# Attention scores with the low key products in two row halves, and the compressed values and the overlap table as one operand

## What is computed

```python
p_c = jax.nn.softmax(jnp.where(mask_c, s_c, NEG_INF), axis=-1) * mask_c
o_cmp = jnp.einsum('bgrqj,bjgd->bqgrd', p_c, vcmp)
...
imp = jnp.einsum('bgrqj,jk->bgqk', p_c, jnp.asarray(overlap.astype(np.float32)))
...
_, sel_idx = lax.top_k(imp, n_pick)
...
s = (jnp.einsum('bqgrd,bgqkd->bgrqk', qb, kg)
     - slopes[None, :, :, None, None] * dist.astype(f32))
p = jax.nn.softmax(jnp.where(dist >= 0, s, NEG_INF), axis=-1)
o_sel = jnp.einsum('bgrqk,bgqkd->bqgrd', p, vg)
...
sw = jnp.einsum('bqgrd,bkgd->bgrqk', qb, kwb) - slopes[..., None, None] * dw.astype(f32)
```

## Time and profile before

| | |
|---|---|
| Time, three runs | 4975.93, 4977.47, 4987.32 us; median 4977.47 |
| Profiled execution | 4984.44 us, of it 4982.9 us from the first to the last instruction |
| TensorE matmul busy | 87% of the span |
| VectorE, ScalarE, GpSimd busy | 55%, 41%, 15% |
| Attention proper | from 2024 to 3077 us of the span |
| TensorE's mean granted clock | 0.922 of full speed |

### The profile page before, as it was taken

One profiled execution on the slowest core, in us unless ns is written; L12 is line 12 of the kernel. 1 busy time (PEld: TensorE's weight loads), 2 busy tenths in 40 slices (PEclk: granted clock), 3 DMA queues, 4 the chain that ended last, 5 costly groups with the idle time before them and its releaser, 6 DMA issues. The chain is left out here.

```text
span 4982.9 us, 66879 instructions
## 1 busy us (share of the span) xinstructions
PE 4327.2 (87%) x24608; PEld 3592.7 (72%) x24609; DVE 2748.0 (55%) x4353; ACT 2039.0 (41%) x3193; POOL 729.3 (15%) x599
## 2 busy tenths in 40 slices
PE   6999999999999995788888876799635999999699
PEld 5887887888788773566666764688534888888577
DVE  2655655556567562576666654443225654557465
ACT  2433332233223221455555553101225655557465
POOL 0111111111122130211111110000012100001110
PEclk9999999999999997899999986899657999999899
DMA  4332322233222214000000001423217865669742
GB/s 138 108 87 74 107 81 62 86 109 87 65 74 61 67 43 104 25 11 14 17 15 17 14 22 55 140 94 115 92 59 293 314 249 214 245 256 344 286 145 98
DMA packets 440438, 558.72 MB, mean 112 GB/s; under 512 B 38908, under 2 KB 299004, under 8 KB 439148
## 3 DMA queue, kind: packets, MB, share of 16 engines
q1 hardware_dynamic: 387892, 451.51, 27.6%
q0 software_dynamic: 19072, 59.86, 3.2%
q10 hardware_dynamic: 33232, 44.10, 2.7%
HBM read 445.05 MB, written 110.35 MB: 111 GB/s over the span
## 5 line engine op out<-in xcount | busy, mean ns | idle before, releaser
L434 POOL TENSOR_TENSOR fr_Lm<-fr_M,fr_join 128x512 f32<-128x512 f32 x224 | 370.9, 1673 | 1493.2 <-DVE fr_M L1043 963.4
L462 PE MATMUL fr_fb<-fr_hT_h,fr_w_h 128*128 128x512 f32 (+1 forms) x1312 | 528.3, 403 | 16.6 <-DVEq L1004 10.8
L462 PE MATMUL fr_fb<-fr_hT_r,fr_w_h 128*128 128x512 f32 (+1 forms) x1312 | 527.4, 402 | 0.0
L462 PE MATMUL fr_fb<-fr_hT_h,fr_w_r 128*128 128x512 f32 (+1 forms) x1312 | 526.3, 401 | 0.0
L855 DVE TENSOR_TENSOR fr_w_r<-fr_w_raw,fr_w_h 128x1024 fp32r<-128x1024 f32 (+1 forms) x164 | 209.6, 1278 | 409.7 <-ACT fr_w_h L683 409.4
L1781 DVE TENSOR_TENSOR aq_p_lo<-aq_t_bank,aq_p_hi 128x512 fp32r<-128x512 f32 x412 | 281.4, 690 | 271.5 <-ACT aq_p_hi L1671 270.1
L1671 ACT CAST aq_p_hi<-aq_t_bank 128x512 fp32r<-128x512 f32 x412 | 238.9, 585 | 377.5 <-PE aq_t_bank L1585 375.4
L707 ACT COPY fr_zs<-fr_fb 128x512 f32<-128x512 f32 (+1 forms) x148 | 87.0, 588 | 585.0 <-PE fr_fb L462 584.6
L462 PEld LDWEIGHTS fr_fb<-fr_hT_h,fr_w_h 128*128 128x128 f32 (+1 forms) x1312 | 246.9, 188 | 74.7 <-DVEq L1004 11.3
L134 PE MATMUL ex_gu<-ex_gate_w,ex_xT 128*128 128x512 f32 x1176 | 288.3, 401 | 11.5 <-DVE ex_xT L2407 11.4
L134 PE MATMUL ex_yps<-ex_down_w,ex_hidT 128*128 128x512 f32 x1176 | 287.6, 400 | 2.6 <-DVE ex_hidT L2423 2.6
(11 more groups left out here) (438 smaller groups left out, 9957.8 us busy)
## 6 DMA issues: line engine op xcount, KB each, us to landing
ex_raw<-in_w_exp_gate_up SPq DMA_DIRECT2D x64, 2048.0 KB, 10.9
fr_w_raw<-in_w_in SPq DMA_DIRECT2D x160, 512.0 KB, 3.8
ex_raw<-in_w_exp_down SPq DMA_DIRECT2D x32, 2048.0 KB, 11.1
s_z<-fr_zs SPq DMA_DIRECT2D x160, 256.0 KB
s_rows<-ex_y ACTq DMA_DIRECT2D x50, 512.0 KB, 4.3
mx_mg<-s_z SPq DMA_DIRECT2D x16, 1024.0 KB, 7.8
fr_zc<-s_z SPq DMA_DIRECT2D x15, 903.0 KB, 6.8
fr_x_t<-in_x SPq DMA_DIRECT2D x16, 512.0 KB, 4.8
```

The costliest lines, as they stand in the source:

```text
L434: pool.tensor_tensor(Lm[:, g, :, :], M[:, 4 * g:4 * g + 4, 0, :], join[:, lev:lev + 1, :].to_broadcast([P, HG, CH]), ALU.mult).then_inc(l_ ...
L462: ins = pe.matmul(bank[0:cols_, :], (w_h, w_h, w_r)[p][:, k, c, 0:cols_].bitcast(F32R), (hT_h, hT_r, hT_h)[p][:, c, :].bitcast(F32R), star ...
```

## The change

**Scores.** A run is always split into two halves by columns, each half in a bank of its own. Both halves are multiplied with `k_hi` as before, with all 128 rows. The products with `k_lo` now use the rounded query alone: half 0 of the columns with rows 0 to 63 of the array, half 1 with rows 64 to 127. A new tile `q_hh` holds the rounded query in all rows for this. `take_q` has one more copy. `mask` reads and writes the two halves with one instruction.

**Fronts.** `overlap` is now part of `vcmp` (two copies, one for each group), so `out` has one product of 96 columns for each head. The sum over heads is made by a `tensor_reduce` in `select`.

**The SEL mask.** `t_sel` is gone. `bias` first adds `sel` to a ramp of one element for each block, then this to the distances within a block (`near`), and masks the last 128 columns with `affine_select`.

```diff
+        CMP_OUT = N_SEL + HD
+        vcmp = kp.sb("vcmp", [P, G, CMP_OUT])
...
+            q_hh = st.sb("q_hh", [P, 2, G, R, P])
...
-                    pool.tensor_copy(whole(q_s, every).bitcast(F32R), raw(every)).then_inc(q_high, 1)
-                    pool.wait_ge(q_high, o + 1)
-                    pool.tensor_tensor(whole(q_s, rest).bitcast(F32R), raw(rest), whole(q_s, rest), ALU.subtract).then_inc(q_ok, 1)
+                    pool.tensor_copy(whole(q_hh, every).bitcast(F32R), raw(every)).then_inc(q_high, 1)
+                    pool.tensor_copy(whole(q_s, top_).bitcast(F32R), raw(top_)).then_inc(q_high, 1)
+                    pool.wait_ge(q_high, 2 * o + 2)
+                    pool.tensor_tensor(whole(q_s, rest).bitcast(F32R), raw(rest), whole(q_hh, rest), ALU.subtract).then_inc(q_ok, 1)
...
+                    pool.tensor_tensor(base[:, 0:blocks], ramp[:, N_SEL - blocks:N_SEL], sel[:, f % SELS, 0:blocks], ALU.add).then_inc(base_ok, 1)
+                    pool.wait_ge(base_ok, 2 * f + 1)
                     pool.tensor_tensor(tg[:, 0:keys].rearrange("p (n b) -> p n b", n=blocks),
-                                       t_sel[:, S - t * P:S - t * P + keys].rearrange("p (n b) -> p n b", n=blocks),
-                                       sel[:, f % SELS, 0:blocks].rearrange("p (n o) -> p n o", o=1).to_broadcast([P, blocks, SEL_BLOCK]),
-                                       ALU.add).then_inc(tg_ok, 1)
+                                       near[:, :].rearrange("p (o b) -> p o b", o=1).to_broadcast([P, blocks, SEL_BLOCK]),
+                                       base[:, 0:blocks].rearrange("p (n o) -> p n o", o=1).to_broadcast([P, blocks, SEL_BLOCK]),
+                                       ALU.add).then_inc(base_ok, 1)
+                    pool.wait_ge(base_ok, 2 * f + 2)
+                    pool.affine_select(out=tg[:, t * P:keys], in_=tg[:, t * P:keys], compare_op=ALU.is_ge, fill=NEG, base=0,
+                                       pattern=[[-1, P]], channel_multiplier=1).then_inc(tg_ok, 1)
...
-                step(pool.memset(overlap[:, :], 1.0))
-                masked(overlap[:, :], [[-4, N_SEL]], 0, 1, 0.5)
...
+                for g in range(G):
+                    overlap = vcmp[:, g, 0:N_SEL]
+                    step(pool.memset(overlap, 1.0))
+                    masked(overlap, [[-4, N_SEL]], 0, 1, 0.5)
...
-                step(pool.iota(t_sel[:, :], [[1, w]], base=-S, channel_multiplier=-1, allow_small_or_imprecise_dtypes=True))
-                masked(t_sel[:, :], [[-1, w]], S, 1, NEG)
+                step(pool.iota(near[:, :], [[1, SEL_BLOCK]], base=0, channel_multiplier=-1, allow_small_or_imprecise_dtypes=True))
+                step(pool.iota(ramp[:, :], [[SEL_BLOCK, N_SEL]], base=P - S, channel_multiplier=0, allow_small_or_imprecise_dtypes=True))
...
                         for h in range(R):
-                            pe.matmul(misc[:, R * HD:R * HD + N_SEL], pct[0:N_CMP, h, :], overlap[0:N_CMP, :],
-                                      start=h == 0, stop=h == R - 1)
-                        for h in range(R):
-                            ins = pe.matmul(misc[:, h * HD:(h + 1) * HD], pct[0:N_CMP, h, :], vcmp[0:N_CMP, k, :], start=True, stop=True)
+                            ins = pe.matmul(misc[:, h * CMP_OUT:(h + 1) * CMP_OUT], pct[0:N_CMP, h, :], vcmp[0:N_CMP, k, :], start=True, stop=True)
...
-                    key = F.low(u) * P + at
-                    for c in range(0, wide, 512):
-                        size = min(512, wide - c)
-                        dst = s_bank[:, i % 2, c:c + size]
-                        for n, k in enumerate((k_hi, k_lo)):
-                            ins = pe.matmul(dst, q_s[:, t % 2, g, h, :].bitcast(F32R),
-                                            k[:, b, g, key + c:key + c + size].bitcast(F32R), start=n == 0, stop=n == 1)
+                    key, half = F.low(u) * P + at, wide // 2
+                    for c in range(2):
+                        pe.matmul(s_bank[:, i % 2, 512 * c:512 * c + half], q_s[:, t % 2, g, h, :].bitcast(F32R),
+                                  k_hi[:, b, g, key + c * half:key + (c + 1) * half].bitcast(F32R), start=True, stop=False)
+                    for c in range(2):
+                        own = slice(c * HD, (c + 1) * HD)
+                        ins = pe.matmul(s_bank[:, i % 2, 512 * c:512 * c + half], q_hh[own, t % 2, g, h, :].bitcast(F32R),
+                                        k_lo[own, b, g, key + c * half:key + (c + 1) * half].bitcast(F32R), start=False, stop=True)
...
-                    dve.tensor_tensor(imp[:, :], misc[:, R * HD:R * HD + N_SEL], keep_t[:, at], ALU.mult).then_inc(imp_ok, 1)
+                    dve.tensor_reduce(imp[:, :], misc[:, 0:R * CMP_OUT].rearrange("p (h n) -> p n h", h=R)[:, 0:N_SEL, :],
+                                      AX.X, ALU.add).then_inc(imp_ok, 1)
                     dve.wait_ge(imp_ok, f + 1)
+                    v.link(dve.tensor_tensor(imp[:, :], imp[:, :], keep_t[:, at], ALU.mult))
...
-                    dve.tensor_tensor_reduce(out=sc_of(u)[:, h, at:at + wide], in0=s_bank[:, i % 2, 0:wide], in1=table,
+                    dve.tensor_tensor_reduce(out=halves(sc_of(u)[:, h, at:at + wide]),
+                                             in0=s_bank[:, i % 2, :].rearrange("p (b n) -> p b n", b=2)[:, :, 0:wide // 2], in1=halves(table),
                                              scale=-SLOPES[g * R + h], scalar=least[:, u % 4, 0, h:h + 1] if at else HIGHEST,
                                              op0=ALU.add, op1=ALU.min, accum_out=slot).then_inc(s_read, 1)
```

More of the change, by code:

```diff
@@ L1380, in _ @@
                 for g in range(G):
-                    dve.tensor_copy(vcmp[0:N_CMP, g, :], out[0:N_CMP, (2 + g) * P:(2 + g) * P + HD]).then_inc(out_ok, 1)
+                    dve.tensor_copy(vcmp[0:N_CMP, g, N_SEL:CMP_OUT], out[0:N_CMP, (2 + g) * P:(2 + g) * P + HD]).then_inc(out_ok, 1)
                 dve.wait_ge(out_ok, 3)
@@ L1388, in stage_nsa @@
             QF, Y = 3, F.Y_RING
-            t_sel, t_win, t_cmp = st.sb("t_sel", [P, S + P]), st.sb("t_win", [P, WK]), st.sb("t_cmp", [P, 256])
+            t_win, t_cmp = st.sb("t_win", [P, WK]), st.sb("t_cmp", [P, 256])
+            near, ramp, base = st.sb("near", [P, SEL_BLOCK]), st.sb("ramp", [P, N_SEL]), st.sb("base", [P, N_SEL])
             rows_ok = st.sb("rows_ok", [P, 1])
             keep_t, force_t = st.sb("keep_t", [P, 64]), st.sb("force_t", [P, 64])
-            overlap, pair = st.sb("overlap", [P, N_SEL]), st.sb("pair", [P, HD])
+            pair = st.sb("pair", [P, HD])
             q_raw = st.sb("q_raw", [P, G, R, P])
             qf, q_s = st.sb("qf", [P, QF, R, P]), st.sb("q_s", [P, 2, G, R, P])
+            q_hh = st.sb("q_hh", [P, 2, G, R, P])
             pc, pct = st.sb("pc", [P, R, P]), st.sb("pct", [P, R, P])
@@ L1414, in stage_nsa @@
                 st.sem(n) for n in ("s_made", "s_read", "exp_ok", "turned", "hi_ok", "lo_ok", "pv_made", "ot_ok"))
-            misc_made, misc_read, cexp_ok, inv_ok, pc_ok, imp_ok, sel_ok, tg_ok, y_ok, vec = (
+            misc_made, misc_read, cexp_ok, inv_ok, pc_ok, imp_ok, sel_ok, tg_ok, y_ok, vec, base_ok = (
                 st.sem(n) for n in ("misc_made", "misc_read", "cexp_ok", "inv_ok", "pc_ok", "imp_ok", "sel_ok",
-                                    "tg_ok", "y_ok", "vec"))
+                                    "tg_ok", "y_ok", "vec", "base_ok"))
             y_out = st.lasting_sem("y_out", Z["whole"])
@@ L1475, in take_q @@
                     whole = lambda a, rows: a[rows, k, :, :, :].rearrange("p g h t -> p (g h) t")
-                    every, rest = slice(0, P), slice(HD, P)
+                    every, top_, rest = slice(0, P), slice(0, HD), slice(HD, P)
                     raw = lambda rows: q_raw[rows, :, :, :].rearrange("p g h t -> p (g h) t")
-                    pool.tensor_copy(whole(q_s, every).bitcast(F32R), raw(every)).then_inc(q_high, 1)
-                    pool.wait_ge(q_high, o + 1)
-                    pool.tensor_tensor(whole(q_s, rest).bitcast(F32R), raw(rest), whole(q_s, rest), ALU.subtract).then_inc(q_ok, 1)
+                    pool.tensor_copy(whole(q_hh, every).bitcast(F32R), raw(every)).then_inc(q_high, 1)
+                    pool.tensor_copy(whole(q_s, top_).bitcast(F32R), raw(top_)).then_inc(q_high, 1)
+                    pool.wait_ge(q_high, 2 * o + 2)
+                    pool.tensor_tensor(whole(q_s, rest).bitcast(F32R), raw(rest), whole(q_hh, rest), ALU.subtract).then_inc(q_ok, 1)
                     pool.wait_ge(q_ok, o + 1)
@@ L1518, in _ @@
                     masked(force_t[half, :], [[1, 64]], -31 - h, 0, 0.0)
-                step(pool.memset(overlap[:, :], 1.0))
-                masked(overlap[:, :], [[-4, N_SEL]], 0, 1, 0.5)
-                masked(overlap[:, :], [[-4, N_SEL]], 1, 1, 0.0)
-                masked(overlap[:, :], [[4, N_SEL]], 2, -1, 0.5)
```

(15 more changed lines are left out.)

4 lines of the change are left out of this document (1 added, 3 removed).

## The result

The changed kernel takes 5061.28 us (median of 4 runs, 5050.15 to 5074.0) against 4976.7 us (4 runs, 4973.06 to 4987.32): a ratio of 1.0167, 95% interval 1.0138 to 1.0197, or +83 us (69 to 98). The forecast was 5019 us and slower, the range 4972 to 5062: the sign was right, the added time is twice the +42 forecast, and the time is inside the range by 0.7 us of its top, which is luck: the interval alone is 14 us to either side. The profiled execution took 5057.94 us, 5056.4 of it the span.

A forecast was written before the change was run, and what follows sets the result against it. TensorE was taken to bound the kernel, its matmuls busy 87% of the span. Scores +49, fronts -23, reduction +3, queries +6, SEL mask +4.5 and start +2.5 gave +42 us on 4977.5: 5019 us, range 4972 to 5062.

The forecast's parts named there:

- scores (halving and row halves): Score runs on TensorE: array switches outweigh the halved k_lo intervals, +76 us of work, +49 us at the end.
- fronts, reduction and their 1.4 of the start: Fronts: eight fewer out matmuls give -23 us, VectorE's reduction +3, the second overlap table at the start 1.4.
- SEL mask: GpSimd's bias: a small add, an affine_select and semaphore waits, 0.65 us each time, +4.5 us (0 to 10).
- queries and their 1.0 of the start: take_q on GpSimd: one more copy of 1.04 us per tile, +6 us, plus one such copy at the start.
- The price of a run: Score run on TensorE: switches cost 0.39 us, less the saved half interval; +0.16 us at 1024 keys, narrow runs lose most.
- rival 4: Score runs: fp32r halves run one after the other, 52 us of half intervals, 0.64 passing: 5052 us; chance 0.05.
- Rival 1: Score runs: the array switches cost nothing, hidden in TensorE's waits or not needed in fp32r: 4931 us; chance 0.08.
- 0.85, 0.35, 0.8, 0.8, together +49 of +76: Shares of added score time reaching the end: WIN 640-wide, SEL tiles 8 to 15, narrow WIN and SEL tiles 0 to 7.
- the mean clock near 0.91: TensorE in the attention: the mean granted clock stays near its 0.91 from before the change.
- rival 3: TensorE's clock falls more often, from fewer columns and more bare gaps: up to +40 us on top, 5059; chance 0.08.
- it lies mostly in TensorE's own stretches: 0.8: Fronts: of the 28.8 us that out saves on TensorE, 0.8 reaches the end, -23 us (-14 to -29).
- The small terms: GpSimd's SEL mask at +4.5 us and the extra query copy at +6 us, plus 1.04 us at the start.

The follow-up runs named there:

- e4: Changed kernel with the k_lo products at all 128 rows again, halves and two banks kept: 5011.65 us, ratio 1.0063 to the kernel before.
- e9: Kernel before with each score run split into halves over two banks, all products at 128 rows, two-bank masks: 4986.73 us, ratio 1.0017.
- e2: Kernel before with only the merged fronts, reduction included: 4989.19 us, ratio 1.0023.
- e3: Kernel before with only the new SEL mask in bias: 4993.41 us, ratio 1.0026.
- e12: Kernel before with only the second query copy in take_q: 4988.65 us, ratio 1.0021.
- e5: Changed kernel with both k_lo halves on rows 0 to 63, so one after the other: 5117.74 us, ratio 1.0267 to the kernel before.
- e6: Kernel before with one extra 64-row matmul of 64 columns ahead of each score run: 5051.75 us, ratio 1.0141.
- e7: Kernel before with one extra 128-row matmul of 64 columns ahead of each score run: 4999.9 us, ratio 1.0037.
- e11: Changed kernel with k_lo products at all 128 rows, plus a 64-row matmul of 64 columns ahead of each run: 5080.89 us, ratio 1.0198 to kernel before.
- e10: Kernel before with merged fronts but no reduction, the selection using head 0's importance alone: 4976.43 us, ratio 0.9995.

## Why the prediction came out as it did

The parts run alone add up to the whole within their intervals: fronts +11, SEL mask +13, halving +9, queries +10, together 43 (31 when joined in `e4`, and the intervals allow for that), and the row halves +52. Against the prediction's terms:

| Term | forecast us | measured us | by |
|---|---|---|---|
| scores (halving and row halves) | +49 | +61 | e9, after less e4 |
| fronts, reduction and their 1.4 of the start | -18.6 | +11 | e2 |
| SEL mask | +4.5 | +13 | e3 |
| queries and their 1.0 of the start | +7 | +10 | e12 |
| joined costs less than the parts | 0 | -12 | e4 |
| sum | +42 | +83 | |

**The price of a run was right.** 1.08 us measured for a run of 1024 keys (0.93 + 0.16 forecast), 0.80 for 640. The halves overlap (rival 4 is wrong: `e5`), the switches cost 0.38 us in fp32r too (0.35 in the run of 640, 0.32 in `e6`), and the loss falls on the narrow runs first. Rival 1, free switches, is wrong by the same rows and by `e6` less `e7`. The Trainium skill, TensorEngine Tiling (Array Packing), "Key Properties", says that a mode change drains the engine; the bare 0.36 and 0.25 us ahead of the weight loads agree.

**The share that passes was wrong.** The step "0.85, 0.35, 0.8, 0.8, together +49 of +76" gives 0.64; `e6` less `e7` gives 0.51 for the switches (52 of 320 x 0.32 us). With it the score term would have been +39. Measured it is +61 of +76, or 0.8. So the switches passed on less than forecast, and more was lost to what the sum left out, the clock above all, which is argued here and not measured apart. That 0.64 lies between the two is luck.

**The clock was wrong.** The step "the mean clock near 0.91" failed; it is 0.86 in the attention. That was rival 3, given 0.08, with the mechanism half right: it named fewer columns and bare gaps. `e11` has the gaps and only 30 of the 80 us at 1.2 GHz that the row halves add. The larger part comes with the products that use half of the rows. The other 82 us of the 162 are there without row halves (`e4`). Its argument against, that around the switches of the projection the paces are those of 2.4 GHz, was drawn from 1.4 us at one place of another stage and could not speak for this one.

How much of the +83 us the clock makes can only be bounded. The Trainium skill, TensorE: Matmul & The Clock Gate, "Terms", puts the penalty of throttled time at that time times one less the granted share, here a half. By that, the 162 us more at 1.2 GHz are up to 81 us, and for the row halves (919 less 839) up to 40 of their 52. Where TensorE sets the pace, as in the three stretches above, it comes near to that: most of their 26 us. Elsewhere a part of it can lie in waits; how much was not measured. The switches are the other large part of the 52, some 50 us by `e6` less `e7`, and by `e11` less `e4` and the dummy; the overlapped columns work against both.

**The fronts were the largest miss: the step "it lies mostly in TensorE's own stretches: 0.8".** `e10` shows a share of about nothing, a third at most by its interval. The prediction's reason was that `out` lies where TensorE is busy 17.3 of 18.0 us. But what follows `out` on TensorE is a `turn` that needs `p_lo`, and VectorE, with the selection of that same front ahead of `p_lo`, sets when it comes. A high busy share in a stretch doesn't say that the work at one point of it is on the path. The reduction, 282 ns by 32 = 9 us with +3 forecast, costs 13, give or take 8: it stands in the one chain on VectorE that `p_lo` queues behind.

**The small terms were too low** by 8 and 3 us. Both were costed by the cover that the profile shows for the typical case. TensorE's waits for `q_s` grew to 9.7 us, not to some 15.

So the sign was right for the reason given, the switches outweigh the halved intervals, though by a smaller share of them than forecast and with the clock beside them, while the sum was half of the true one: fronts 30 us off, scores 12, mask and queries 11, less 12 for the joined parts. No kernel of this study is faster than the one before; `e10`, which leaves work out, equals it.

## What to carry to other kernels

Before splitting a contraction of 64 over the array's halves, price the change of mode (0.32 to 0.38 us for there and back here) against the interval saved for each visit. One pair a visit lost here at every width; whether more pairs standing together would pay was not tried. Look at the granted clock too: here it fell with half-row matmuls. Before TensorE work is counted as saved at the end, look at what the next TensorE instruction waits for when it comes earlier; a busy share of a stretch is no answer. An instruction added to a chain in which another engine's next step queues, as the reduction here, can cost all of itself, however idle its engine is on average.

## What the hardware showed that was not expected

- With equal columns, counts and banks, half-row products in place of full-row ones (`e5` for `e4`) take the mean granted clock of an execution from 0.916 to 0.904; as many switches without them (`e11`) take it to 0.915. The two kernels also differ in the numbers that are multiplied (`e4` has the rest of the query in rows 64 to 127), and that was not tested apart. Why was not shown; the profile gives the clock, not its cause.
- GpSimd's cast of 1024 elements takes 1036 ns on 64 partitions and 1039 ns on 128.
- A mask on VectorE that reads two banks and writes one row is as fast as one that reads a contiguous one: 1223 ns for 1024 columns, 816 for 640.
- A VectorE reduction of 128 x 128 to 128 x 32 with stride, from PSUM, takes 282 ns, as long as the one of 128 x 128 to 128 x 16 in the earlier trace rows.
